# Turning the next tile of x by transposing DMAs in place of TensorE, in a fused DeltaNet and sliding-window layer

## What is computed

```python
h = rmsnorm(x, pre_norm_w)
proj = einsum('bsd,de->bse', h, w_in)              # 1024 -> 3336 columns
(qa, ka, va, za, ba, aa, qb, kb, vb, zb) = split(proj)
qkv = silu(causal_depthwise_conv(concat([qa, ka, va]), conv_w))
o_a = rmsnorm(gated_deltanet(qkv, ...)) * silu(za)  # 4 heads x 128, chunks of 64
o_b = sliding_window_sink_attention(rope(qb), rope(kb), vb, sinks) * silu(zb)
y = einsum('bse,ed->bsd', concat([o_a, o_b]), w_out)
out = x + rmsnorm(y, post_norm_w)
```

## Time and the profile before

| | |
|---|---|
| median of 3 runs | 2064.43 us (2063.4 to 2065.26) |
| profiled execution, its own time | 2063.36 us |
| its span, first to last instruction | 2061.6 us |
| TensorE busy | 1993.6 us, 97% |
| VectorE busy | 1606.6 us, 78% |
| ScalarE busy | 996.5 us, 48% |
| GpSimd busy | 562.0 us, 27% |
| mean granted TensorE clock | 0.985 |
| one tile in the steady part | 61.42 us |

### The profile page before, as it was taken

One profiled execution on the slowest core, in us unless ns is written; L12 is line 12 of the kernel. 1 busy time (PEld: TensorE's weight loads), 2 busy tenths in 40 slices (PEclk: granted clock), 3 DMA queues, 4 the chain that ended last, 5 costly groups with the idle time before them and its releaser, 6 DMA issues.

```text
span 2061.6 us, 56696 instructions
## 1 busy us (share of the span) xinstructions
PE 1993.6 (97%) x22625; PEld 1563.5 (76%) x22625; DVE 1606.6 (78%) x5421; ACT 996.5 (48%) x3144; POOL 562.0 (27%) x839
## 2 busy tenths in 40 slices
PE   7589999999999999999999999999999999999995
PEld 6367777788777788778788778788777778877773
DVE  6898777788777778777778777778777778877775
ACT  6655444545454545454545444444544454545442
POOL 0222223232323232323233223223222323232321
PEclk9799999999999999999999999999999999999997
DMA  9001100111110111110111110011111011111001
GB/s 358 31 24 55 45 25 23 44 45 45 45 35 18 40 45 45 45 35 24 33 45 45 45 43 22 26 45 45 45 45 30 18 44 45 45 45 35 21 26 43
DMA packets 40010, 93.79 MB, mean 45 GB/s; under 512 B 13577, under 2 KB 17986, under 8 KB 39746
## 3 DMA queue, kind: packets, MB, share of 16 engines
q1 hardware_dynamic: 39314, 90.16, 13.5%
q10 hardware_dynamic: 432, 0.01, 0.0%
HBM read 71.28 MB, written 18.87 MB: 44 GB/s over the span
## 4 chain that ended last, share of the span: by engine, by line
PE 91%; DVE 4%; ACT 2%; issue 1%; DMA 0%; SPq 0%; POOL 0%; DVEq 0%; POOLq 0%; ACTq 0%
PE bank L510 32%; PE bank L517 19%; PE bank L608 15%; PE bank L525 10%; PE bank L590 2%; PE bank L721 2%; PE bank L582 1%; PE bank L445 1%; DVE w_raw L1586 1%; PE bank L542 1%; PE bank L565 1%; PE bank L547 1%; ACT w_raw L1045 1%; PE bank L668 1%; DVE qkv L1119 1%
## 5 line engine op out<-in xcount | busy, mean ns | idle before, releaser
L510 PE MATMUL bank<-xt_half,w_raw 128*128 128x128 f16 x11904 | 731.3, 219 | 0.0
L510 PEld LDWEIGHTS bank<-xt_half,w_raw 128*128 128x128 f16 x11904 | 692.3, 98 | 28.2 <-issue 5.2
L517 PE MATMUL bank<-w_raw,xt_half 128*128 128x512 f16 (+1 forms) x2232 | 433.0, 346 | 11.6 <-ACT xt_half L816 9.6
L1119 DVE SCALAR_TENSOR_TENSOR qkv<-conv_in,cols,qkv 128x128 f32<-128x128 f32 x1152 | 391.7, 383 | 3.5
L517 PEld LDWEIGHTS bank<-w_raw,xt_half 128*128 128x128 f16 x2232 | 218.2, 98 | 171.7 <-issue 11.5
L608 PE MATMUL bank<-w_o,inv_t 128*128 128x512 f16 x768 | 171.0, 379 | 2.0 <-DVE inv_t L1315 2.0
L608 PE MATMUL bank<-w_o,out_b_half 128*128 128x512 f16 x762 | 171.1, 381 | 0.0
L1117 DVE TENSOR_SCALAR qkv<-conv_in,cols 128x128 f32<-128x128 f32 x384 | 90.8, 281 | 86.3 <-ACT halo L850 85.1
L608 PEld LDWEIGHTS bank<-w_o,inv_t 128*128 128x128 f16 x768 | 73.7, 98 | 85.5 <-DVE inv_t L1315 2.4
L608 PEld LDWEIGHTS bank<-w_o,out_b_half 128*128 128x128 f16 x762 | 73.5, 98 | 83.1 <-issue 1.1
L816 ACT ACTIVATE xt_half<-bank,small 128x128 f16<-128x128 f16 x496 | 131.2, 415 | 3.8 <-DVE small L1630 3.6
(11 more groups left out here) (260 smaller groups left out, 3541.5 us busy)
## 6 DMA issues: line engine op xcount, KB each, us to landing
x_in<-in_x_dram SPq DMA_DIRECT2D x32, 512.0 KB, 3.5
x_in<-near_scratch SPq DMA_DIRECT2D x32, 512.0 KB, 4.5
y_out<-in_x_dram SPq DMA_DIRECT2D x32, 512.0 KB, 3.5
out_dram<-y_out SPq DMA_DIRECT2D x31, 512.0 KB, 3.0
w_raw<-in_w_in_dram SPq DMA_DIRECT2D x8, 768.0 KB, 10.5
w_raw<-in_w_in_dram SPq DMA_DIRECT2D x16, 256.0 KB, 10.6
w_o<-in_w_out_dram SPq DMA_DIRECT2D x8, 512.0 KB, 12.0
w_raw<-in_w_in_dram SPq DMA_DIRECT2D x8, 384.0 KB, 10.7
```

The costliest lines, as they stand in the source:

```text
L510: last = mm(dst[:, 128 * b:128 * b + 128], w_half[:, c, ws, col:col + 128], xt_half[:, xs, c, :], start=(c == 0 and ws + xs == 0), stop=(c ...
L517: last = mm(dst[:, 0:n_col], xt_half[:, xs, c, :], w_half[:, c, ws, col:col + n_col], start=(c == 0 and ws + xs == 0), stop=(c == NC - 1 a ...
L1119: last = v.scalar_tensor_tensor(dst, conv_in[:, b, i:i + TOK], tap, dst, ALU.mult, ALU.add)
```

## The change

`turn_x` and its PSUM banks go. In its place SP, once both halves of the tile are written and `FILL_Q` has read the old tile, issues four transposing DMAs straight from `x_half` to `xt_half`: for each half i of the channel blocks, one for the high and one for the low parts, each of 128x512 float16 (128 KB). ScalarE then multiplies the row factors in place, eight instructions of 128x256 (a block's high and low part together) in place of sixteen of 128x128. It signals after every second block, and each piece of `FILL_ZA` waits only for its own pair of blocks. `finish` gets a wait for the transposing DMAs, since it overwrites `x_half`. TensorE's transposes of k no longer wait for the copy of x. The rest renames semaphores: one of them is saved by letting `pool_link` serve twice, so its counts go up by one.

```diff
+        def flipped_x(eng, n, parts=range(2)):
+            for i in parts:
+                eng.wait_ge(x_flipped[i], 32 * n)
+
+        def turned_x(eng, t, pair=3):
+            eng.wait_ge(xt_ready, NC + 4 * (t - 1) + pair + 1)
...
+            def flip_x(n):
+                done(sp, xl_ready, n - 1)
+                if n > 1:
+                    done(sp, fill_ready[FILL_Q], n - 1)
+                for i in range(2):
+                    for s in range(2):
+                        at = NC // 2 * i
+                        sp.dma_start_transpose(xt_half[:, s, at:at + NC // 2, :],
+                                               x_split(n)[:, s, 128 * at:128 * at + 64 * NC]).then_inc(x_flipped[i], 16)
...
                 if not mix:
+                    flip_x(1)
...
                 if prep and mix:
                     done(sp, to_ready, m)
                     sp.dma_start(x_in[:, :], x[0, bass.ds((t + 1) * TOK, TOK), :]).then_inc(x_loaded, 16)
+                if prep and mix:
+                    flip_x(t + 1)
...
-            def turn_x(n):
-                done(pe, xh_ready, n)
-                done(pe, w_ready, n - 2)
-                done(pe, o_ready, n - 2)
-                for s in range(2):
-                    if s:
-                        done(pe, xl_ready, n - 1)
-                    dst = bank[6 + s][:, :].bitcast(F16).rearrange("p (c n) -> p c n", c=NC)
-                    for c in range(NC):
-                        last = nc.tensor.transpose(dst[:, c, :], x_split(n)[:, s, 128 * c:128 * c + 128], ident16)
-                last.then_inc(x_turned, 1)
...
-                turn_x(1)
...
-                        if (f, b) == (0, 0):
-                            turned_x(pe, t)
+                        if f == FILL_ZA:
+                            turned_x(pe, t, b)
...
-                turned_x(pe, t if proj else m)
...
-                if prep:
-                    turn_x(t + 1)
...
             def copy_xt(n):
-                done(act, x_turned, n)
                 if n == 1:
                     act.wait_ge(w_range_ready, 1)
-                else:
-                    done(act, fill_ready[FILL_Q], n - 1)
-                for s in range(2):
-                    src = bank[6 + s][:, :].bitcast(F16).rearrange("p (c n) -> p c n", c=NC)
-                    for c in range(NC):
-                        last = f(xt_half[:, s, c, :], src[:, c, :], ACT.Identity, scale=x_factor[:, c:c + 1])
-                last.then_inc(xt_ready, 1)
+                for c in range(NC):
+                    if c % (NC // 2) == 0:
+                        flipped_x(act, n, [2 * c // NC])
+                    last = f(xt_half[:, :, c, :], xt_half[:, :, c, :], ACT.Identity, scale=x_factor[:, c:c + 1])
+                    if c % 2:
+                        last.then_inc(xt_ready, 1)
...
             def finish(m):
                 done(dve, y_rs_ready, m)
+                flipped_x(dve, min(m + 2, NT - 1))
```

More of the change, by code:

```diff
@@ L241, in build @@
             sem(n) for n in ("wo_scale_ready", "wo_hi_ready", "wo_lo_ready", "wo_ready", "setup_turned", "heads_loaded"))
-        setup_link, neg_a_exp, pool_set = (sem(n) for n in ("setup_link", "neg_a_exp", "pool_set"))
-        x_sq_ready, x_rs_ready, xh_ready, xl_ready, x_turned, xt_ready = (
-            sem(n) for n in ("x_sq_ready", "x_rs_ready", "xh_ready", "xl_ready", "x_turned", "xt_ready"))
+        setup_link, neg_a_exp = (sem(n) for n in ("setup_link", "neg_a_exp"))
+        x_sq_ready, x_rs_ready, xh_ready, xl_ready, x_first_turned, xt_ready = (
+            sem(n) for n in ("x_sq_ready", "x_rs_ready", "xh_ready", "xl_ready", "x_first_turned", "xt_ready"))
+        x_flipped = sems("x_flipped", 2)
         fill_ready = sems("fill_ready", 7)
@@ L293, in build @@
             sem(n) for n in ("y_ready", "y_sq_ready", "y_rs_ready", "y_used", "post_ready"))
-        def turned_x(eng, t):
-            eng.wait_ge(xt_ready, NC + t)
+        def flipped_x(eng, n, parts=range(2)):
[3 more added lines that the diff above has]
+            eng.wait_ge(xt_ready, NC + 4 * (t - 1) + pair + 1)
         fill_used = {FILL_ZA: gate_a_ready, FILL_V: conv_in_ready[2], FILL_KVB: kv_raw_ready,
@@ L472, in first_fills @@
                 turn_tops(w_top[:, 0:2], 1)
-                done(pe, conv_in_ready[2], 0)
-                done(pe, kv_raw_ready, 0)
-                turn_x(1)
             def turn_tops(tops, n):
@@ L787, in _ @@
                                            x_first[:, 128 * c:128 * c + 128], ident)
-            last.then_inc(x_turned, 1)
+            last.then_inc(x_first_turned, 1)
             run_steps(pe, step)
@@ L831, in w_out_high @@
                     act.wait_ge(wo_scale_ready, 1)
-                    done(act, x_turned, 1)
+                    flipped_x(act, 1)
                 c = OUT_ORDER[i]
@@ L887, in query_raw @@
                 if t == 0:
-                    done(act, x_turned, 0)
+                    done(act, x_first_turned, 0)
                 f(shared[:, 0:512], fill_bank(t, FILL_QB)[:, :], ACT.Identity, scale=1.0 if t == 0 else unscale).then_inc(
@@ L1342, in last_mix @@
                     o_argument()
-                    dve.wait_ge(pool_link, m * 3 + 1)
+                    dve.wait_ge(pool_link, m * 3 + 1 + 1)
                     done(dve, o_gated, m)
@@ L1569, in _ @@
             link(v.tensor_single_scalar(norm_abs.bitcast(I32), cols[:, 48:56].bitcast(I32), 0x7FFFFFFF, ALU.bitwise_and))
-            done(dve, x_turned, 0)
+            done(dve, x_first_turned, 0)
             for c in range(NC):
@@ L1687, in _ @@
             g.memset(root_scale, X_SCALE * D ** 0.5)
-            g.memset(power[:, 8:16], 0.5).then_inc(pool_set, 1)
-            pool.wait_ge(pool_set, 1)
+            g.memset(power[:, 8:16], 0.5).then_inc(pool_link, 1)
+            pool.wait_ge(pool_link, 1)
             def rotate(dst, src, swap, n):
@@ L1750, in step @@
                     g.tensor_tensor(o_f, o_f, (out_f_first if m == 0 else out_f).broadcast_to([128, 4]), ALU.mult).then_inc(pool_link, 1)
-                    pool.wait_ge(pool_link, m * 3 + 1)
+                    pool.wait_ge(pool_link, m * 3 + 1 + 1)
                     done(pool, o_gated, m)
@@ L1756, in step @@
                     g.tensor_tensor(y_arg, y_sq[:, 0:1], eps_y, ALU.add).then_inc(pool_link, 1)
-                    pool.wait_ge(pool_link, m * 3 + 2)
+                    pool.wait_ge(pool_link, m * 3 + 1 + 2)
                     done(pool, y_sq_ready, m if proj else m + 1)
                     g.tensor_tensor(y_arg, y_arg, y_sq[:, 1:2], ALU.add).then_inc(pool_link, 1)
-                    pool.wait_ge(pool_link, m * 3 + 3)
+                    pool.wait_ge(pool_link, m * 3 + 1 + 3)
                     g.tensor_tensor(y_rs, y_arg, power[:, 0:1], ALU.pow).then_inc(y_rs_ready, 1)
```

## The result

The changed kernel takes 2181.18 us (median of 4 runs, 2179.64 to 2183.17), the kernel before beside it 2064.85 (2063.4 to 2066.34): ratio 1.0564, 95% interval 1.055 to 1.0577. It is 116 us slower. I had forecast 2047.4 and a range to 2150. The profiled execution took 2179.64 us, its span is 2177.8.

What follows compares the result with a forecast made beforehand. TensorE, busy 61.42 us of each 61.42 us tile, was taken to bound the kernel. Per tile -0.89 + 0.33 = -0.56 us, over 29 tiles 16, plus 1 from the start-up: -17, so 2047.4 us, range 2034 to 2150.

Steps and rivals of the forecast that it cites:

- The slack of 0.40 us for `y_used`: Before the first Gram product: time `y_used` has to spare once the transposes go, down from 1.29 us.
- the tanh as what is queued behind the copies: On ScalarE: tanh and both squares wait behind the copies; tanh slips from T+5.42 to T+6.15 (T: end of `FILL_Q`).
- the wait at the Gram product: On TensorE: the only new wait in the steady part, 0.33 us a tile.
- the `FILL_ZA` pieces: On TensorE: pieces of x come in time, the first pair ready at T+3.9 and wanted at T+6.5; no wait.
- the 0.89 us freed per tile: On TensorE: the 16 transposes per tile go, freeing 25.8 us over 29 tiles if no wait opens.
- full gain: Per tile: all of the 0.89 us kept, for a DMA pace up to 0.37 us.
- rival 1: DMAs hidden: pace no more than a plain issue, 0.33 us, all 0.89 us a tile kept, 2037 us; chance 0.15.
- the pace of the DMAs: On SP's queue: 0.68 us per transposing DMA, issue (0.59) and movement (0.68) side by side; nothing gained at 0.93.
- My own formula: Landing of the k-th DMA at T+2.4+(k-1)p; copies end at the later of T+2.4+p+3.05 and T+2.4+3p+1.52.
- Rival 2: Issuing queue handles each block like its own DMA: slower, 2098 us at 0.33 a block, 2190 at 0.59; chance 0.33.
- The copies: On ScalarE: eight of 128x256 at 0.38 us each, 3.05 us in all, bounds 2.1 to 4.2.
- the rival with gaps of 24 us: Blocks go one at a time with full latency: TensorE idles 24.5 us per tile, about 2750 us; chance 0.07.

Runs made afterwards that it cites:

- experiments 1: Changed kernel with ScalarE's tanh and squares of y put ahead of the last four copies: 2042.52 us, 0.9892 of the kernel before.
- experiment 2: Changed kernel with the transposing DMAs writing to idle `x_in` before `FILL_Q` ends, ScalarE copying from there to `xt_half`: 2037.67 us, 0.9869 of the kernel before.
- Experiment 3: Changed kernel with four plain DMAs of the same bytes, not transposing (projections from unturned x): 2047.47 us, 0.9916 of the kernel before.
- Experiment 5: Changed kernel with eight transposing DMAs of two 128x128 blocks each in place of four of four: 2326.96 us (one run).
- 7: Changed kernel with fewer, larger transposing DMAs: one of sixteen blocks 2096.47 us; two of eight 2135.92; one, with tanh and squares before the last four copies, 2051.99.
- experiment 4: Changed kernel with one more DMA behind the fourth: a 512-byte one to memory, 2188.22 us; a fifth transposing one into `x_in`, 2180.81 us.
- 6: Changed kernel with 15 matmuls that nobody reads per tile, in front of the Gram products: 2136.69 us, 1.0346 of the kernel before.

## Why the prediction was wrong

**What bounds the kernel, and where the change would bite: right.** The slack of 0.40 us for `y_used`, the tanh as what is queued behind the copies, the wait at the Gram product and none to speak of at the `FILL_ZA` pieces, the 0.89 us freed per tile: experiments 1 and 2 bear it out. With the waits gone the tile is 60.4 us (60.5 forecast for full gain), and the time 2037.67 is rival 1's 2037.

**The step that failed is the pace of the DMAs.** I took p, the time from one DMA to the next, as 0.68 us, the larger of an issue of 0.59 (the row of a plain DMA with 256-byte rows) and 0.68 of movement. The issue of a transposing DMA measured 1.27 us, 1.30 from start to start. Experiment 3 shows that the arrangement was worth what I said and the operation was not. My own formula with p = 1.30 gives a landing at T+6.3 (6.45 measured in the early tiles) and an idle time of 2.0 us (2.17 measured): that alone makes it slower than before.

**Rival 2 gave the right sign, for a wrong reason.** It priced the issue per block of 128x128, 1.32 us for four, and so came near the measured 1.30 by accident. Experiment 5 shows the same 1.25 for two blocks, 7 shows 1.31 for eight and 1.9 for sixteen. By the rival's reason, fewer blocks per DMA would have been harmless; in fact it cost 146 us more.

**Three terms were missing.** The sum of the changed kernel against experiment 2, spans: 2177.8 - 2036.0 = 141.8. Of it 84.9 are idle at the Gram product and 53.4 longer instructions; 3.5 are left for smaller waits. Of the idle time, 29 x 2.17 and 0.6 in tile 2, together 63.5, belong to the pace of the issues and the copies, and 15 x 1.43 = 21 to the late landing in every second tile. Of the longer instructions 45 are the lower clock after gaps of 2 to 4 us and 8 the start after a wait. None of the three was in any price; I had named the clock only beside the rival with gaps of 24 us. Together they are 75 us, and they carry the result past my range's end of 2150.

**The copies:** 1.70 us for four in place of 1.5 (0.41 a copy, 0.38 taken). A small part.

**The rules I had weighed.** For the same 128 KB the queue is held 1.27 us by a transposing DMA and 0.60 by a plain one, so the rule of the Trainium skill that transposing DMAs on TRN2 are as fast as plain ones (Advanced Engine Details and Errata, X-Bar Transpose) does not hold for four of this size. For 512 KB in one, landing after 4.4 us against 3.5 for a plain load of x from memory, it is nearer. The issue hardly goes by the size up to eight blocks; so the 32 cycles a tile that I had taken from the Trainium skill's DMA: Bandwidth & Descriptors (its table of sequencer cycles) for an estimate of 0.85 us do not describe it either.

**The late landing.** It is not the last place in the row (experiment 4), nor the number of DMAs or their bytes: one or two DMAs with the same 512 KB have landed before the next load starts. It goes with the instruction loads. In the changed kernel and experiments 1, 2, 4 (the 512-byte DMA) and 6, which have four transposing DMAs a tile, such a load starts ahead of the fourth landing in 75 of 150 tiles; the landing comes after 6.6 to 8.4 us in all of these and after 6.4 to 6.5 in all others, and experiments 2 and 6 moved the loads against the DMAs and the late tiles moved with them. With the fifth DMA there is one tile in which the load starts at 6.3 us; there the fourth lands in time and the fifth late.

**What stays open.** No run is without the loads, so that they cause the lateness is argued from this agreement. The load itself takes about 1 us, and the landing is told another 1.0 to 1.2 us after the last packet; why that is not 0.4, as in an early tile, nothing here tells. Nor does it tell why the clock falls after some gaps and not after others of the same length.

## What to carry to other kernels

Price a DMA of a kind that the trace doesn't hold by its issue on the queue as well as by its bytes, and take a range of issue up to three times that of a plain one; count the DMAs, for here each cost 1.25 to 1.31 us whatever its size up to eight blocks. Where a landing is late at regular intervals, look for instruction loads in the list of the DMA queues. When a step moves to an engine that waits for a DMA, what stands behind it on that engine's list is the cost: putting three instructions ahead of the wait took 139 us off this kernel. And price a new gap on a TensorE that had none at more than its length: here 85 us of gaps brought 53 us of slower work, 45 by the clock and 8 by the start after each wait.

## What the hardware showed that I had not expected

- A transposing DMA between two places in SBUF: issue 1.25 us for 2 blocks of 128x128 float16, 1.27 for 4, 1.31 for 8, 1.6 to 2.5 for 16; landing 2.4, 2.5, 3.3 and 4.4 us after the start of the issue. A plain one of the size of 4 blocks: 0.60 and 2.1.
- A landing 1.5 to 2 us later than in the other tiles wherever a 16 KB load of instructions started 5.8 to 6.2 us after the first issue, near the end of the fourth DMA's data: 15 of the 30 tiles.
- Gaps of 1.7 us in 29 tiles (one of them 2.1) left TensorE's clock at 1.00; with two DMAs, gaps of 1.9 were followed by 3.4 us at 0.50 in 20 of 30 tiles, some 34 us in all. In the changed kernel gaps of 2.2 were followed by 3.4 us of it in 8 of 14 tiles, and gaps of 3.6 by 3.4 or 6.8 us in 13 of 15.
- A Gram product that has waited takes 0.27 us more than one that follows without a gap, at the same clock: 2.05 against 1.78.
